# Attention scores of two heads computed from their own 64 partitions, in one call for both heads

## The reference

```python
proj = u @ w_in                                     # q, k, v of both groups
s = einsum(q, k) * HEAD_DIM ** -0.5                 # per head, over the 64 elements of the head
p = softmax(s + bias)                               # masked where outside the window
o = einsum(p, v)
```

## Time and profile before

| | |
|---|---|
| time, median of 3 runs | 2241.8 us (2241.23 to 2241.85) |
| profiled execution: its own time / its span | 2241.42 us / 2239.6 us |
| mean granted TensorE clock | 0.965 of full speed |
| attention phases of groups A and B | about 844 to 1144 us and 1144 to 1408 us of the span |
| scoring stretches, group A | about 16 units x 4 head pairs, from 879, 953, 1028 and 1101 us |
| scoring stretches, group B | the same, from 1182, 1247, 1313 and 1380 us |

### The profile page before, as it was taken

One profiled execution on the slowest core, in us unless ns is written; L12 is line 12 of the kernel. 1 busy time (PEld: TensorE's weight loads), 2 busy tenths in 40 slices (PEclk: granted clock), 3 DMA queues, 4 the chain that ended last, 5 costly groups with the idle time before them and its releaser, 6 DMA issues. The chain is left out here.

```text
span 2239.6 us, 27243 instructions
## 1 busy us (share of the span) xinstructions
PE 2040.5 (91%) x10350; PEld 1585.9 (71%) x10350; DVE 1100.8 (49%) x1891; ACT 753.1 (34%) x1253; POOL 462.5 (21%) x332
## 2 busy tenths in 40 slices
PE   3999999999999938999988889794999999999997
PEld 2777777777888826766666666673888888878885
DVE  4854544454346473344324443467743444443556
ACT  2533323333223243244323433315433333332331
POOL 0622222220004120000033202231622222100041
PEclk6999999999999969999999999897999999999998
DMA  6253444444644021100133021503222222265341
GB/s 254 82 160 124 157 156 130 155 142 168 246 147 167 30 104 47 57 28 29 56 82 60 19 49 38 197 38 120 76 89 74 90 80 90 90 237 195 141 168 49
DMA packets 157608, 247.34 MB, mean 110 GB/s; under 512 B 8097, under 2 KB 106673, under 8 KB 157361
## 3 DMA queue, kind: packets, MB, share of 16 engines
q1 hardware_dynamic: 126370, 211.36, 27.3%
q10 hardware_dynamic: 30096, 30.25, 4.4%
q0 software_dynamic: 1024, 4.13, 1.2%
HBM read 205.09 MB, written 40.63 MB: 110 GB/s over the span
## 5 line engine op out<-in xcount | busy, mean ns | idle before, releaser
L1280 PE MATMUL f_ps<-f_uh,f_ops 128*128 128x512 f32 x2496 | 794.1, 395 | 9.0 <-DVE acc L1119 4.9
L1280 PEld LDWEIGHTS f_ps<-f_uh,f_ops 128*128 128x128 f32 x2496 | 470.5, 188 | 137.8 <-issue 28.0
L1280 PE MATMUL f_ps<-f_ul,f_ops 128*128 128x512 f32 x1248 | 491.1, 394 | 0.0
L1380 PE MATMUL f_ps<-f_wdh,f_hdh 128*128 128x512 f32 x704 | 273.9, 389 | 0.0
L1380 PE MATMUL f_ps<-f_wdl,f_hdh 128*128 128x512 f32 x704 | 273.9, 389 | 0.0
L1380 PE MATMUL f_ps<-f_wdh,f_hdl 128*128 128x512 f32 x704 | 273.9, 389 | 0.0
L1280 PEld LDWEIGHTS f_ps<-f_ul,f_ops 128*128 128x128 f32 x1248 | 235.4, 189 | 48.2
L1180 DVE TENSOR_TENSOR f_wdl<-f_wd,f_wdh 128x2048 fp32r<-128x2048 f32 x44 | 107.3, 2438 | 227.2 <-ACT f_wdh L1010 227.2
L868 POOL TENSOR_TENSOR f_sums<-f_raw 128x512 f32<-128x512 f32 x80 | 107.4, 1343 | 444.4 <-DVE f_ops L1080 359.8
L1080 DVE TENSOR_TENSOR f_ops<-f_sums,f_ops 128x512 fp32r<-128x512 f32 x160 | 118.6, 741 | 153.9 <-ACT f_ops L906 153.9
L1010 ACT CAST f_wdh<-f_wd 128x2048 fp32r<-128x2048 f32 x44 | 83.9, 1907 | 302.5 <-PE f_ps L1380 259.5
(11 more groups left out here) (212 smaller groups left out, 2652.2 us busy)
## 6 DMA issues: line engine op xcount, KB each, us to landing
f_wd<-in_ffn_w_down SPq DMA_DIRECT2D x44, 1024.0 KB, 4.9
f_raw<-in_ffn_w_gate SPq DMA_DIRECT2D x22, 1024.0 KB, 5.5
f_raw<-in_ffn_w_up SPq DMA_DIRECT2D x22, 1024.0 KB, 5.4
f_hidden<-acc SPq DMA_DIRECT2D x88, 256.0 KB, 2.2
f_hd<-f_hidden SPq DMA_DIRECT2D x44, 512.0 KB, 5.6
f_aw<-in_w_ada ACTq DMA_DIRECT2D x28, 512.0 KB, 3.6
acc<-in_w_ada ACTq DMA_DIRECT2D x28, 512.0 KB, 3.5
in_raw<-in_w_in SPq DMA_DIRECT2D x24, 512.0 KB, 6.7
```

Source lines behind the costliest of these rows:

```text
L1280: done = nc.tensor.matmul(ps[:, bank, :], l[:, k, :], r[:, k, :], start=fresh and k == 0 and m == 0, stop=closed and k == HK - 1 and m == ...
L1380: done = nc.tensor.matmul(ps[:, b, :], l[n % 3][:, c, P * t:P * t + P], r[n % 3][:, c, NB * (b % 2):NB * (b % 2) + NB], start=p == 0 and c ...
```

## The change

`score(p, m, first)`, called for each unit, becomes `scores(p, m, first)`, called for each even m. It issues the matmuls of both heads of the query tile. Each matmul reads only the 64 partitions of its own head (`rows`), of the queries and of the keys, so the contraction is over 64 rows of the array and not over 128. Head 0 writes bank 0, head 1 bank 1, as before. The call waits until both banks have been read, `low` of units m-2 and m-1. In group A the class matmuls of the two heads alternate, and `qk` is raised for each head at its last class. The number of matmuls is the same. The zeros are still written into `q`.

```diff
-            def score(p, m, first):
-                u, b = NU * p + m, m % 2
-                t, i = m // 2, m % 2
+            def scores(p, m, first):
+                u, t = NU * p + m, m // 2
                 if not (first and m < 2):
-                    pe.wait_ge(low, u - 1)
+                    pe.wait_ge(low, u)
                 if dil:
                     w0 = band_start(t)
-                    nc.tensor.matmul(sc[:, b, 0:BAND], q[:, i, P * t:P * t + P], kv[:, 0, w0:w0 + BAND],
-                                     start=True, stop=True, skip_group_check=True)
+                    for i in range(2):
+                        rows = slice(HD * i, HD * i + HD)
+                        nc.tensor.matmul(sc[:, i, 0:BAND], q[rows, i, P * t:P * t + P], kv[rows, 0, w0:w0 + BAND],
+                                         start=True, stop=True, skip_group_check=True)
                     for r in range(CL):
-                        last = nc.tensor.matmul(sc[CQ * r:CQ * r + CQ, b, BAND:BAND + CK],
-                                                q[:, i, P * t + CQ * r:P * t + CQ * r + CQ], kc[:, r, :],
-                                                start=True, stop=True, skip_group_check=True)
+                        for i in range(2):
+                            rows = slice(HD * i, HD * i + HD)
+                            last = nc.tensor.matmul(sc[CQ * r:CQ * r + CQ, i, BAND:BAND + CK],
+                                                    q[rows, i, P * t + CQ * r:P * t + CQ * r + CQ], kc[rows, r, :],
+                                                    start=True, stop=True, skip_group_check=True)
+                            if r == CL - 1:
+                                last.then_inc(qk, 1)
                 else:
                     cb, rb = t // RBS, t % RBS
                     grid = kv[:, 0, :].rearrange("p (r c) -> p r c", c=COLS)
-                    last = nc.tensor.matmul(sc[:, b, 0:W], q[:, i, P * t:P * t + P],
-                                            grid[:, 4 * rb:4 * rb + KR, KC0[cb]:KC0[cb] + KC],
-                                            start=True, stop=True)
-                last.then_inc(qk, 1)
+                    for i in range(2):
+                        rows = slice(HD * i, HD * i + HD)
+                        nc.tensor.matmul(sc[:, i, 0:W], q[rows, i, P * t:P * t + P],
+                                         grid[rows, 4 * rb:4 * rb + KR, KC0[cb]:KC0[cb] + KC],
+                                         start=True, stop=True, skip_group_check=True).then_inc(qk, 1)
...
                 for m in range(NU + LAG):
-                    if m < NU:
-                        score(p, m, first)
+                    if m < NU and m % 2 == 0:
+                        scores(p, m, first)
                     if m >= LAG:
                         turn(p, m - LAG, first)
```

## The result

The changed kernel takes 2281.98 us (median of 4 runs, 2277.1 to 2284.28), the kernel before 2241.52 us. The ratio is 1.0182 (95% interval 1.0166 to 1.0198), or 40.8 us. The sign was right; the size is four times the forecast 10.2 us and lies outside the range of 2243 to 2273. The profiled execution took 2284.28 us, its span is 2282.5 us, its mean granted clock 0.939 against 0.965.

A forecast was written before the change was run, and what follows sets the result against it. TensorE was taken to pace group A, a loop with no full engine group B. Losses of 3.3 (A), 5.9 (B) and 1.0 us (clock) sum to 10.2, giving 2252 us; own range 2247 to 2257, 8-in-10 range 2243 to 2273.

The forecast's parts named there:

- (1) Two heads at once: Scores: row halves overlap fully, relieving TensorE of some 1.09 us per two units in group A, 0.64 in B.
- Rival A: Scores: row halves overlap only partly or not at all, +10 or +21 us, 2262 or 2273 us; chance 0.16.
- (2) The bank wait: Waiting for both banks exposes scoring latency; two-unit loops of 3.28 (A) and 2.52 us (B); costs 3.3 and 5.9 us.
- (3) Shape changes: Array reshaped more often, also between turns and scores; some 0.1 us each, counted as nothing because covered.
- (4) The clock: Longer TensorE idle time during group B's splits brings one more clock fall, 1 us (bounds 0 and 2 x 1.7).
- rival C: Clock stays low in group B, about 1.2 us on five loops in four pairs, +24, 2276 us; chance 0.05.
- rival B: Scoring latency shorter than thought: no change or faster, even at 0.21 us less per latency; chance 0.24.

The follow-up runs named there:

- e1: Changed kernel plus idle 128x512 matmuls on the full array between the two turns of each pair of units; 2248.03 us, ratio 1.0041.
- e3: Kernel before, but both heads scored in one call behind the new bank wait, each over all 128 rows, one after the other; 2254.51 us, ratio 1.0064.
- e4: Changed kernel with three banks for the scores in place of two, and one for the output; 2261.84 us, ratio 1.0093.
- e5: Changed kernel with three score banks and idle matmuls on all 128 rows; 2242.77 us, ratio 1.0008.
- e2: Kernel before, old order and old bank wait, with score operands cut to the head's 64 partitions; 2337.77 us, ratio 1.0444.
- e9: Kernel before with one tiny matmul (64 rows, 16 columns) ahead of each unit's scores, which keep all 128 rows; 2275.73 us, ratio 1.0147.
- e7: Changed kernel's scoring in group A alone, group B scored as in the kernel before; 2262.57 us, ratio 1.0099.
- e8: Changed kernel plus idle matmuls between the turns that read 64 rows in place of 128; 2251.61 us, ratio 1.0056.
- e10: Changed kernel with three score banks, scores issued ahead of the turns, a third buffer for divided tiles, and idle matmuls; 2223.03 us, ratio 0.991.

## Why the prediction was right and wrong

**(1) Two heads at once: right.** Full overlap, 0.70 us for both heads' bands. Rival A fell: neither one pass (0.21 us) nor two more are in the band. The Trainium skill's statement that row groups run concurrently ("TensorE: Matmul & The Clock Gate", Part 3) agrees with the trace, by these 0.70 us.

**(2) The bank wait: right in its place and its loops, somewhat too large in its cost.** Latency 1.39 (forecast 1.39), loops 3.27 and 2.50 (3.28 and 2.52). The cost is about 7 us for 9.2 forecast: in e1's trace A's stretch is 3.0 us longer than before (forecast 3.3) and B's 5.2, of which 2.1 are e1's own matmuls (forecast 5.9). The sum for B also took `low` of unit 1 at the start of its read, 1183.97, and not at its end, 1184.05; that is 0.3 us over four pairs. That TensorE's saving would be off the path is what e3, e4 and e5 show: with the old amount of matmul work e3 is 0.6% slower, and with the bank wait gone the next wait in line, the queue behind a turn, keeps e5 at 1.0008.

**(3) Shape changes: nothing on the path here, as forecast,** since the latency came out at 1.39. Uncovered, with the load that isn't made ahead, they cost some 0.2 us each: e2's unit takes 1.77 for 1.59 us with one more, e9's 1.99 with two more and a small matmul. The forecast had 0.1.

**(4) The clock: the term that failed.** I had it at 1.0 us, bounds 0 and 3.4, from a single fall after 2.9 us of idle time. It is 31 to 34 us: 40.8 measured, less the 9.2 of e1 or the 7 of the bank wait alone. The failed reasoning is in rival C: "it fell only after idle time near 3 us". That sentence read the one fall of the earlier trace rows as the rule. In the changed kernel the second band of pair 0 already runs at the lower level, 1.23 us long, after idle times of 0.78 and 1.47 us:

```profile
880.52 0.70 PE L1788 MATMUL a_sc<-a_kv,a_q 64*128 64x256 f32 x4 [0.78 <-DVE a_q L1521]
...
883.28 1.23 PE L1788 MATMUL a_sc<-a_kv,a_q 64*128 64x256 f32 x4 [1.47 <-DVE a_sm L1686]
```

In e2 it fell and stayed low while TensorE hardly paused. Falls behind the idle time of a split do happen as well (before, e3, e7, e9), but cost a few us at most. Rival C had the right mechanism and nearly the right loop for B (3.7 us for 3.53 measured), but was given 0.05, and only for B, while A loses about as much (19.5 us for 22.3).

A slip besides: the bounds named for the forecast's own range add up to 2250 to 2259, not to 2247 to 2257. And the 0.39 us of rival B for the depth of the array has no working from rows; since the latency is 1.39, nothing hangs on it.

**What pulls it down.** In the changed kernel both halves of the array work in the scores, and there is time without work: filled with full matmuls (e1) or half-filled ones (e8), the clock stays up. In e2 there is hardly such time, but half-filled scores: 0.85 and 0.81. The wait with the old amount of work (e3) and the shape changes with full scores (e9) leave the clock of the loops where it was. Both ways to the lower level have in common that the array has less to do than before. That reading is argued and not shown, and it is no rule: e8 too gives the array less to do than the kernel before and kept the clock, and most of one pair of e2 ran at the higher level with the same instructions. What decides stays open. Rival B fell: the latency is 1.39, no shorter than forecast.

## What to carry to other kernels

Before you count saved TensorE time as won, ask what the loop's next limit is and whether double buffering survives the new order; here 1.09 us per two units were saved and a scoring latency became exposed instead. Where TensorE's work shrinks inside a loop that another engine paces, price the whole loop at both clock levels (3.27 and 4.61 us) and give the lower one a real chance, whatever the busy share says. Here the cut in matmul work paid only when the freed time was put on the path (e10: banks, buffers and order together), and a few idle matmuls were cheaper than the lower clock (e1).

## What the hardware showed that I had not expected

- Matmuls that fill half the array's rows, in a stream without a pause (busy 10.00 of 10 us), ran at a granted clock of 0.50 (e2); the stream of e9, as full and with the rows filled by zeros, held 1.00. In these runs TensorE's speed thus depended on how the operands are laid out.
- Adding matmuls that nobody uses took 31 us off the changed kernel: 2281.98 us beside 2241.52 for the kernel before, 2248.03 beside 2238.9 with them.
- The same instructions ran at either level: in e2 pair 1 of group A at 0.50 and pair 2 at 1.00, units of 3.19 and 1.77 us.
